# Hosting four input-projection loads instead of two in the first attention of a two-block layer, with the modulation sums read in half-megabyte pieces

## The chip, the cores and the metric

The kernel runs on one core of one Trainium2 chip. The metric is the device time of one execution in microseconds (us), as the median over runs. Three runs of the kernel before gave 2601.82, 2596.1 and 2588.16 us.

## The reference

Two blocks run on 256 tokens of width 2048, in float32. The change lies in the first one:

```python
mod = c_act @ ada_w + ada_b                      # 2048 x 12288: 24 loads of 512 columns
sh1, sc1, g1, sh2, sc2, g2 = split(mod, 6)
u = rms_norm(h, norm_mix_g) * (1.0 + sc1) + sh1
proj = u @ w_in                                  # split into q, k, v, gates of four attentions
o = concat([fox_attention, nsa_attention, dilated_attention, diff_attention])
h = h + g1 * (o @ w_out)
u = rms_norm(h, norm_ffn_g) * (1.0 + sc2) + sh2
h = h + g2 * swiglu(u, ffn_w_gate, ffn_w_up, ffn_w_down)
x = rms_norm(h, final_norm_g)
```

Fox has 7 heads with a cumulated forget gate, the dilated attention (DIL) 9, NSA 8 with three branches (cmp, slc, win) whose results are added under gates, and the differential attention (DIFF) 4 heads of two maps each. A second block (memory attention, chunked attention, an RWKV-like mixer) follows and is not changed.

## The kernel before

**Weights and units.** A weight matrix is cut into loads of 2048 rows by 512 columns (4 MB), a load into four units of 1 MB. SP brings the units in the order of `STREAM` (line 102) into a ring of four; ring slot g is loaded again when unit g is done (line 1760). Every float32 product is made of three: ACT rounds the unit to its high half (`high`, line 1858), DVE subtracts for the low half (`low`, line 2530), and PE takes high x high, high x low and low x high (`unit`, line 2127, with tokens in PSUM rows, 24 products of 512 columns; `unit_features`, line 2143, with features in rows, 48 products of 256 columns). The last third of a unit waits for its low half (line 2136 or 2150).

**Dense stage.** `W_IN_ORDER` (line 98) has the twelve loads of w_in. The first `N_DENSE` = 10 are run one after the other (line 2246). Loads 0 to 7 are feature loads: 0 and 1 fox and dilated queries, 2 NSA queries, 3 DIFF queries, 4 and 5 the keys of 0 and 1, 6 DIFF keys, 7 the NSA keys. Loads 8 to 11 are token loads (gates and values); of load 11 only 288 columns are used (line 95). Beside the units PE makes the compress products of NSA (line 2231).

**ada.** `mod` comes from 24 ada loads: DVE multiplies 16 rows of 128x512 by a scalar of c each and adds them up (`ada_part`, line 2538), and PE sums over partitions with `ada_sum` (line 2183, 8 short instructions). The first `N_FIRST_ADA` = 8 loads come before w_in; POOL fetches them, and the ninth, into two buffers of 4 MB, in halves of 2 MB (line 1783). The loads 8 to 16 use one buffer of 4 MB beside the dense units (line 1803), 4.5 rows in each slot, a slot being the time of one unit from the second load on (lines 227 to 230, 2675). The next three (`N_MID`) come in pieces of two rows (0.5 MB), one buffer, beside the attention: POOL sends a piece when the one before is used (line 1811), `ada_pieces` (line 2563) takes it in the steps of `MID_PIECE` (line 233). The four last run beside the FFN.

**POOL's queue.** In order: the early ada halves, mem to DRAM, cmp_w1 (lines 1797 to 1802, when the 16th transpose round is done), the ada halves of loads 9 to 16, both parts of the mask tables (line 1807), the pieces (line 1809). cmp_w1 is 2 MB, the tables of DIL and cmp 2.1 MB, those of NSA and DIFF 1.6 MB.

**First attention.** `GROUP_SEQ` (line 79) lists seven groups for each of two query tiles: 0 and 1 fox and dilated, 2 slc, 3 win, 4 cmp, 5 and 6 DIFF; 48 units of two heads. In step n (line 2390) PE runs the hosted products of that step, the scores of unit n, the transposes of the probabilities of unit n-2 and the values of unit n-3. DVE (line 2823) adds the mask table and takes the maximum (`score`, L2706, L2710), ACT takes the exponentials; the scores of unit n wait for DVE's L2710 of unit n-1. The planner `plan_hosted` (line 192) spreads the hosted units over the steps by `STEP_MM` (line 189) and with them the halves of their high and low conversions (L2806). Hosted are loads 10 and 11 of w_in and of w_out the half that needs only the fox and dilated heads, which is transposed in steps 20 to 23 (`FD_ROUNDS`). `finish` (line 2729) reads a group's bank four steps after its end. Two rounds of transposes for DIFF run at steps 48 and 49, those for NSA after the loop (line 2432), then the other half of w_out (line 2428 on) and the FFN.

Of the kernel before, what the change touches and what calls it, by code (L numbers as in the profile page):

```python
# [5 lines left out]
P = 128  # L6
SEQ = 256
# [21 lines left out]
N_ADA, N_EARLY, N_FIRST_ADA, N_MID = 24, 17, 8, 3  # L29
# [21 lines left out]
def place(table, *items):  # L51
    at = 0
    for name, n in items:
# [25 lines left out]
GROUP_SEQ = ([(qt, g) for qt in range(TT) for g in (1, 0)] + [(0, g) for g in (2, 3, 4, 5, 6)]  # L79
             + [(1, g) for g in (2, 5, 6, 3, 4)])  # L80
# [17 lines left out]
W_IN_ORDER = (7, 8, 0, 1, 2, 3, 4, 5, 6, 9, 10, 11)  # L98
N_DENSE = 10
# [86 lines left out]
HOSTED_UNITS = [(i, q, 4) for i in range(2) for q in range(4)] + [(2 + nb, q, 2) for nb in range(4) for q in range(2)]  # L186
LAST_HOSTED = HOSTED + len(HOSTED_UNITS)
N_STEPS = N_ATT + 3
STEP_MM = [12] * 8 + [6] * 16 + [7] * 24 + [8] * 3
# [37 lines left out]
ADA_COUNT = [(k + 1) * 9 // 2 - k * 9 // 2 for k in range(32)]  # L227
ADA_END = [next(k for k in range(32) if (k + 1) * 9 // 2 >= 16 * (m + 1)) for m in range(N_EARLY - N_FIRST_ADA)]
ADA_SUM_SLOT = {k + 2: N_FIRST_ADA + m for m, k in enumerate(ADA_END)}
ADA_READ_SLOT = {k + 4: N_FIRST_ADA + m for m, k in enumerate(ADA_END)}  # L230


MID_PIECE = {(2 * i if i < 12 else 26 + (i - 12) * 18 // 11): i for i in range(8 * N_MID)}
MID_SUM = {n + 2: N_EARLY + i // 8 for n, i in MID_PIECE.items() if i % 8 == 7}
FD_ROUNDS, DIFF_ROUNDS = (20, 21, 22, 23), (48, 49)
# [106 lines left out]
def hybrid_blocks(nc, A, out):  # L342

    ctx = ExitStack()
    with ctx:
# [19 lines left out]
        def ada_buf(i):  # L365

            if i % 2 == 0 and i < N_EARLY or N_EARLY <= i < N_EARLY + N_MID:
                return ada_acc
            return ada_tmp[:]

        def ada_bank(i):

            if N_EARLY <= i < N_EARLY + N_MID:
                return TRB
            return OB if i < N_FIRST_ADA or i >= N_EARLY else TRB + 1
# [67 lines left out]
        def ada_piece(i):  # L443

            if i < 12:
                return xn[:, 0, 1024:2048].rearrange("p (k n) -> p k n", n=CH)
            at = xT_flat[:, 3072:4096] if i < 8 * N_MID else xn_flat[:, 2048:3072]
            return at.rearrange("p (k n) -> p k n", n=CH)
# [41 lines left out]
            "tabs_in0", "tabs_in1", "w1_in", "early_in0", "early_in1", "early_in2", "early_in3", "early_used", "mem_saved", "piece_in", "piece_used", "gate_exp", "gate_done", "f_abs", "f_ln", "logf_ready",  # L490
# [16 lines left out]
        def early_of(n):  # L507

            if n >= N_FIRST_ADA:
                return early, 0, N_FIRST_ADA // 2 + n - N_FIRST_ADA  # L510
            return (early2 if n % 2 else early), 2 * (n % 2), n // 2
# [4 lines left out]
        DIFF_AT = [GROUP_END[GROUP_SEQ.index((qt, 6))] + 6 for qt in range(TT)]  # L516
# [94 lines left out]
        def probT(n):  # L611

            at = xn[:, 1, 1024:2048] if n < 36 else xT_flat[:, 2048:3072]
# [1161 lines left out]
        def _(pool):  # L1775

            def early_half(n, half):
                k = slice(half * KT // 2, (half + 1) * KT // 2)
                return pool.dma_start(early[:, k], A["ada_early"][n, half].rearrange("p (k n) -> p k n", n=CH))


            pool.dma_start(mem_x[:, 0], A["mem"][0:P]).then_inc(s_["mem_in"], 16)
            for n in range(N_FIRST_ADA + 1):
                buf, which, _ = early_of(n)
                for half in range(2):
                    if n >= 2:
# [3 lines left out]
                        .then_inc(s_[f"early_in{which + half}"], 16)  # L1790
            def early_loads(first, last):
                with pool.Fori(first, last) as n:
                    for half in range(2):
                        pool.wait_ge(s_["early_used"], n * 2 + (half - 1))
                        early_half(n, half).then_inc(s_[f"early_in{half}"], 16)

# [6 lines left out]
            early_loads(N_FIRST_ADA + 1, N_EARLY)  # L1803

            n_tabs = A["tabs"].shape[1]
# [1241 lines left out]
```

## Time and profile before

| what | value |
|---|---|
| median of three runs | 2596.1 us |
| profiled execution | 2601.68 us |
| its span, first to last instruction | 2599.9 us |
| mean granted clock of TensorE in it | 0.981 |
| instructions | 35147 |
| DMA | 549.44 MB, mean 211 GB/s |

The span is what the rows below are cut from; 1.8 us lie around it. PE is TensorE's matmuls, PEld its weight loads, DVE VectorE, ACT ScalarE, POOL GpSimd, SP SyncE. Granted clock 1.00 is 2.4 GHz, 0.50 is 1.2 GHz; a stretch between the two has parts of both. The reported end of a matmul is modelled and overlaps the next start, so a group's pitch is read from start to start.

### The profile page before, as it was taken

Reading aid. Unit: us, or ns where it says so; the run is one execution under the profiler, and the core shown is the slowest. Engines: PE = TensorE matmul, PEld = TensorE weight load, DVE = VectorE, ACT = ScalarE, POOL = GpSimd, SP = SyncE. Lnnn points to the kernel's source line nnn. Section 1 sums busy time; section 2 is a strip of 40 time slices with the busy share of each in tenths; the row PEclk is TensorE's granted clock in tenths of the full one; section 3 lists DMA queues with packets and bytes.
Section 4 is the critical chain, followed back from the end, with each engine's and each line's share of the span. In section 5 each row is a group of like instructions: output and inputs, shape, how many; then the busy total and the mean of one; then the engine's idle time right before and its main releaser. Section 6 shows DMA issues by size and latency. Waiting matters only on the chain.

```text
span 2599.9 us, 35147 instructions
## 1 busy us (share of the span) xinstructions
PE 2520.6 (97%) x15126; PEld 2030.0 (78%) x15126; DVE 1568.6 (60%) x1843; ACT 1025.7 (39%) x1246; POOL 88.1 (3%) x162
## 2 busy tenths in 40 slices
PE   6999999889899999999999899999999999999999
PEld 3479997767688888888888788887888777777887
DVE  6778884666755555555444665546954454446864
ACT  2033334445443333333333444543654333333332
POOL 0000000000000000000000000001000000000000
PEclk9999999789899999999999999999999999999999
DMA  9988995333366666655555654456655333335654
GB/s 409 427 303 315 349 359 208 123 129 132 135 225 223 229 222 226 226 213 208 179 193 194 251 184 147 177 206 213 226 185 188 125 125 121 127 131 219 253 184 162
DMA packets 77802, 549.44 MB, mean 211 GB/s; under 512 B 8807, under 2 KB 8967, under 8 KB 22737
## 3 DMA queue, kind: packets, MB, share of 16 engines
q1 hardware_dynamic: 56656, 405.36, 43.2%
q0 software_dynamic: 20992, 141.85, 14.4%
q8 instruction: 119, 1.95, 0.3%
q14 instruction: 35, 0.28, 0.0%
HBM read 531.46 MB, written 12.58 MB: 209 GB/s over the span
## 4 chain that ended last, share of the span: by engine, by line
PE 90%; DVE 5%; DMA 3%; ACT 1%; issue 1%; SPq 0%; DVEq 0%; ACTq 0%
PE psum L2138 40%; PE psum L1015 25%; PE psum L2153 7%; PE psum L2211 4%; PE psum L2371 2%; PE psum L2121 2%; DMA weights<-in_loads 1%; DMA xT<-in_loads 1%; PE psum L1143 1%; PE psum L1152 1%; PE psum L1150 1%; PE psum L2193 1%; PE psum L2290 1%; PE psum L2312 1%; DVE arena L2577 1%
## 5 line engine op out<-in xcount | busy, mean ns | idle before, releaser
L1828 ACT ACTIVATE unit_high<-weights 128x1024 fp32r<-128x1024 f32 (+1 forms) x501 | 717.6, 1448 | 1098.7 <-PE psum L2138 612.9
L2533 DVE TENSOR_TENSOR unit_low<-weights,unit_high 128x2048 fp32r<-128x2048 f32 x229 | 524.6, 2291 | 441.3 <-ACT unit_high L1828 440.9
L1388 DVE TENSOR_TENSOR unit_low<-weights,unit_high 128x1024 fp32r<-128x1024 f32 x240 | 289.2, 1221 | 188.8 <-ACT unit_high L1828 188.7
L2138 PE MATMUL psum<-unit_high,z_high 128*128 128x512 f32 x1152 | 290.7, 395 | 1.8 <-DVE arena L2870 1.8
L2138 PE MATMUL psum<-unit_high,z_low 128*128 128x512 f32 x1152 | 284.7, 389 | 0.0
L2138 PE MATMUL psum<-unit_low,z_high 128*128 128x512 f32 x1152 | 284.6, 389 | 0.0
L1015 PE MATMUL psum<-unit_high,z_high 128*128 128x512 f32 x960 | 284.6, 406 | 0.0
L1015 PE MATMUL psum<-unit_high,z_low 128*128 128x512 f32 x960 | 266.9, 394 | 0.0
L1015 PE MATMUL psum<-unit_low,z_high 128*128 128x512 f32 x960 | 263.8, 396 | 1.3 <-DVE unit_low L1388 1.3
L2138 PEld LDWEIGHTS psum<-unit_high,z_high 128*128 128x128 f32 x1152 | 215.8, 190 | 46.4 <-DVE arena L2870 2.2
L2138 PEld LDWEIGHTS psum<-unit_high,z_low 128*128 128x128 f32 x1152 | 216.2, 188 | 45.3
L2138 PEld LDWEIGHTS psum<-unit_low,z_high 128*128 128x128 f32 x1152 | 216.2, 188 | 44.9
L1015 PEld LDWEIGHTS psum<-unit_high,z_low 128*128 128x128 f32 x960 | 179.5, 188 | 40.8 <-issue 1.4
L1015 PEld LDWEIGHTS psum<-unit_low,z_high 128*128 128x128 f32 x960 | 176.3, 188 | 39.6 <-DVE unit_low L1388 2.1
L1015 PEld LDWEIGHTS psum<-unit_high,z_high 128*128 128x128 f32 x960 | 170.9, 188 | 36.0 <-issue 2.0
L1828 ACT ACTIVATE xn<-psum 128x256 f32<-128x256 f32 (+2 forms) x96 | 41.9, 437 | 214.7 <-PE psum L1143 126.5
L2211 PE MATMUL psum<-weights,arena 128*128 128x512 f32 x256 | 115.0, 607 | 6.4 <-DMA weights<-in_loads 5.4
L2555 DVE SCALAR_TENSOR_TENSOR arena<-arena,misc 128x512 f32<-128x512 f32 x135 | 101.4, 751 | 6.4 <-DMA arena<-in_ada_early 1.9
L2211 PEld LDWEIGHTS psum<-weights,arena 128*128 128x128 f32 x256 | 49.0, 194 | 65.4 <-issue 58.7
L1828 ACT ACTIVATE arena<-psum 128x512 f32<-128x512 f32 (+6 forms) x113 | 62.0, 577 | 65.6 <-PE psum L2211 48.9
L2138 PE MATMUL psum<-unit_high,h_high 128*128 128x512 f32 x352 | 87.5, 391 | 0.0
L2138 PE MATMUL psum<-unit_low,h_high 128*128 128x512 f32 x352 | 86.9, 389 | 0.0
(405 smaller groups left out, 2817.0 us busy)
## 6 DMA issues: line engine op xcount, KB each, us to landing
weights<-in_loads SPq DMA_DIRECT2D x380, 1024.0 KB, 4.8
arena<-in_ada_early POOLq DMA_DIRECT2D x26, 2048.0 KB, 11.3
xn<-in_loads POOLq DMA_DIRECT2D x44, 512.0 KB, 5.3
weights<-in_ada_early POOLq DMA_DIRECT2D x8, 2048.0 KB, 21.3
xT<-in_loads POOLq DMA_DIRECT2D x12, 512.0 KB, 3.9
gates_kept<-h POOLq DMA_DIRECT2D x12, 512.0 KB, 3.5
arena<-gates_kept POOLq DMA_DIRECT2D x12, 512.0 KB, 8.5
arena<-in_b_rows POOLq DMA_DIRECT2D x10, 512.0 KB, 6.9
```

What stands on the lines that cost most here:

```text
L1015: ins = mm(psum[:, FILL_BANKS[j % 3]], x[:, 4 * q + k, m * P:(m + 1) * P], w[:, k], start=(q == 0 and i in (0, 12)), stop=(q == 3 and i in ...
L1143: ins = mm(psum[r, 4, u * DH:(u + 1) * DH], Lm[r, u], DD[r, u, 0], start=True, stop=True)
L1150: mm(psum[r, 5, u * C2:u * C2 + DH], DD[r, u, 1], Pm[r, u], start=True, stop=True)
L1388: ins = V.tensor_tensor(ring_lo[:, g % RING, c], ring[:, g % RING, c], unit_hi[:, g % 2, c].bitcast(F32), ALU.subtract)
L1828: return nc.scalar.activation(out_, in_, ACT.Copy, scale=scale)
L2121: ins = nc.tensor.transpose(psum[:, bank, (2 * j + m) * P:(2 * j + m + 1) * P], src[:, m, k * P:(k + 1) * P], ident)
L2138: ins = mm(psum[:, bank + m, 0:width], xk[:, m * P:(m + 1) * P], w[:, k, 0:width], start=(first and i % 8 in (0, 4) and part == 0), stop=( ...
L2153: ins = mm(psum[:, bank + c // 2, (c % 2) * SEQ:(c % 2 + 1) * SEQ], w[:, k, c * P:(c + 1) * P], x[:, k0 + k], start=(first and part == 0 a ...
L2211: ins = mm(psum[:, 2 * (i % 2) + m], memT[:, 4 * q + k, m * P:(m + 1) * P], w[:, k], start=(q == 0 and k == 0), stop=(q == 3 and k == 3), ...
L2371: ins = mm(psum[:, FILL_BANKS[j % 3], 0:width], x[:, 4 * q + k, m * P:(m + 1) * P], w[:, k, 0:width], start=(q == 0 and u in (0, 12)), sto ...
L2533: V.tensor_tensor(ring_lo[:, g % RING], ring[:, g % RING], unit_hi[:, g % 2].bitcast(F32), ALU.subtract)\
L2555: ins = V.scalar_tensor_tensor(acc_, early[:, k], c_act[:, k:k + 1], acc_, ALU.mult, ALU.add)
```

## The change

It hosts four loads of w_in (10, 11, 3, 6) instead of two, and so has eight dense loads; the hosted feature loads are computed with features in rows, two products of 256 columns in place of one of 512. `STEP_MM` becomes twelve products in steps 0 to 31, nine in 32 to 47, eight in 48 to 50 and 24 in a new last step 51. The order of groups is now fox and dilated for both tiles, then (0, cmp), (0, slc), (0, win), (1, slc), (1, win), the four DIFF groups and (1, cmp); `NSA_FIRST` names the branch that writes instead of adding. The transposes for the fox and dilated half of w_out move to steps 28 to 31, those for DIFF to step 50. `N_EARLY` is 8: the ninth early load and the 4 MB buffer are gone, and from the eighth load on all ada rows come as pieces of 0.5 MB: 65 of them (2 or 3 in a slot) beside the dense units, one in each of steps 0 to 14 and 32 to 47, through three buffers. These lie in the first 12 KB per partition of the table area, so POOL loads the tables of DIL and cmp before the pieces and those of NSA and DIFF after piece 79; then the pieces wait for the last hosted unit of w_in and use three other buffers.

```diff
-N_ADA, N_EARLY, N_FIRST_ADA, N_MID = 24, 17, 8, 3
+N_ADA, N_EARLY, N_MID = 24, 8, 12
...
-GROUP_SEQ = ([(qt, g) for qt in range(TT) for g in (1, 0)] + [(0, g) for g in (2, 3, 4, 5, 6)]
-             + [(1, g) for g in (2, 5, 6, 3, 4)])
+GROUP_SEQ = [(0, 1), (0, 0), (1, 1), (1, 0), (0, 4), (0, 2), (0, 3), (1, 2), (1, 3), (0, 5), (0, 6), (1, 5), (1, 6), (1, 4)]
+NSA_FIRST = (4, 2)
...
-W_IN_ORDER = (7, 8, 0, 1, 2, 3, 4, 5, 6, 9, 10, 11)
-N_DENSE = 10
+W_IN_ORDER = (7, 8, 0, 1, 4, 5, 2, 9, 10, 11, 3, 6)
+N_DENSE = 8
...
-N_STEPS = N_ATT + 3
-STEP_MM = [12] * 8 + [6] * 16 + [7] * 24 + [8] * 3
+N_STEPS = N_ATT + 4
+STEP_MM = [12] * 32 + [9] * 16 + [8] * 3 + [24]
...
+SLOT_PIECE = [range(k * 65 // 28, (k + 1) * 65 // 28) for k in range(28)]
+MID_PIECE = {**{n: 65 + n for n in range(15)}, **{32 + k: 80 + k for k in range(16)}}
+ADA_END = [next(k for k in range(28) if 8 * m + 7 in SLOT_PIECE[k]) for m in range(8)]
+ADA_SUM_SLOT = {min(k + 2, 27): N_EARLY + m for m, k in enumerate(ADA_END)}
...
-FD_ROUNDS, DIFF_ROUNDS = (20, 21, 22, 23), (48, 49)
+FD_ROUNDS = (28, 29, 30, 31)
...
-            if i < 12:
-                return xn[:, 0, 1024:2048].rearrange("p (k n) -> p k n", n=CH)
-            at = xT_flat[:, 3072:4096] if i < 8 * N_MID else xn_flat[:, 2048:3072]
+            if i < 80:
+                at = arena[:, 12288 + i % 3 * 1024:12288 + (i % 3 + 1) * 1024]
+            elif i < 8 * N_MID:
+                at = (xT_flat[:, 3072:4096], Wb[:, 1, 3 * UNIT:3 * UNIT + 1024], Wb[:, 1, 3 * UNIT + 1024:4 * UNIT])[i % 3]
+            else:
+                at = xn_flat[:, 2048:3072]
...
             n_tabs = A["tabs"].shape[1]
+            a = N_ALIBI * TAB_W
             pool.wait_ge(s_["early_used"], 2 * N_EARLY)
-            for half, (a, b) in enumerate(((N_ALIBI * TAB_W, n_tabs), (0, N_ALIBI * TAB_W))):
-                nc.gpsimd.dma_start(arena[:, 12288 + a:12288 + b], A["tabs"][:, a:b]).then_inc(s_[f"tabs_in{half}"], 16)
+            nc.gpsimd.dma_start(arena[:, 12288 + a:12288 + n_tabs], A["tabs"][:, a:n_tabs]).then_inc(s_["tabs_in0"], 16)
             for i in range(N_PIECES):
-                if i:
+                if i == 80:
+                    pool.wait_ge(s_["piece_used"], 80)
+                    nc.gpsimd.dma_start(arena[:, 12288:12288 + a], A["tabs"][:, 0:a]).then_inc(s_["tabs_in1"], 16)
+                    pool.wait_ge(s_["unit_done"], HOSTED + 4 * len(HOSTED_LOADS))
+                elif i >= 8 * N_MID:
                     pool.wait_ge(s_["piece_used"], i)
-                else:
-                    pool.wait_ge(s_["cmp_hidden"], 1)
-                if i == 12:
-                    pool.wait_ge(s_["unit_done"], unit_of(PLAN["w_in"][0] + 11, 3) + 1)
+                elif i >= 3:
+                    pool.wait_ge(s_["piece_used"], i - 2)
...
+                if (qt, p) == (0, GROUPS[5][0]):
+                    pe.wait_ge(s_["hosted_free"], 8)
...
+                        if load is not None and load < 8:
+                            for c in range(2):
+                                cs = slice((2 * m + c) * P, (2 * m + c + 1) * P)
+                                ins = mm(bank[:, c * SEQ:(c + 1) * SEQ], w[:, k, cs], x[:, 4 * q + k],
+                                         start=(first and c == 0), stop=last, skip_group_check=True)
...
+                if n == N_ATT + 2:
+                    pe.wait_ge(s_["o_ready"], 2)
+                    pe.wait_ge(s_["pt_ready"], N_ATT)
+                    pe.wait_ge(s_["mod_ready"], N_EARLY + N_MID + 1)
+                    pe.wait_ge(s_["pv_read"], len(GROUP_SEQ) - 1)
+                    transposes(o, KT // 4, 12)
...
-                    if slot < len(ADA_COUNT):
-                        ada_run(ADA_COUNT[slot])
+                    for i in SLOT_PIECE[slot]:
+                        ada_pieces(i)
```

## Rows read from the trace of the kernel before

**Rows 1.** The page: busy time of TensorE, and the chain that ended last, by engine.

```profile
PE 2520.6 (97%) x15126; PEld 2030.0 (78%) x15126; DVE 1568.6 (60%) x1843; ACT 1025.7 (39%) x1246; POOL 88.1 (3%) x162
...
PE 90%; DVE 5%; DMA 3%; ACT 1%; issue 1%; SPq 0%; DVEq 0%; ACTq 0%
```

**Rows 2.** Busy time by stage: us, each engine's busy us, clock, DMA share, GB/s.

```profile
284.00:372.00 88.00, 88.00 (x738) 88.00 (x738) 78.81 (x84) 33.15 (x23) 4.25 (x8) 1.00 0.95 369
372.00:409.00 37.00, 37.00 (x227) 33.28 (x226) 21.48 (x18) 12.41 (x7) 1.57 (x3) 1.00 0.81 313
409.00:452.00 43.00, 41.61 (x216) 31.53 (x214) 22.09 (x64) 20.73 (x53) 2.12 (x4) 0.92 0.49 171
452.00:500.00 48.00, 45.22 (x230) 36.23 (x228) 24.52 (x72) 19.01 (x55) 2.65 (x5) 0.72 0.29 98
500.00:520.00 20.00, 14.80 (x105) 12.54 (x104) 16.17 (x53) 12.35 (x38) 1.59 (x3) 0.91 0.48 166
520.00:560.00 40.00, 35.04 (x170) 25.32 (x172) 23.32 (x72) 16.32 (x53) 2.12 (x4) 0.86 0.34 117
560.00:600.00 40.00, 33.94 (x199) 25.16 (x201) 26.92 (x81) 22.17 (x52) 3.19 (x6) 0.97 0.43 145
600.00:631.00 31.00, 30.45 (x180) 23.85 (x179) 21.72 (x61) 19.82 (x50) 0.53 (x1) 0.95 0.31 103
631.00:700.00 69.00, 56.45 (x237) 44.59 (x237) 49.81 (x55) 30.51 (x40) 0.00 (x0) 0.90 0.39 137
```

**Rows 3.** Waits from 409 to 631 us: who for whom, total us, times, longest.

```profile
DVE arena L2577 <- DMA xT<-in_loads: 15.3, 5, 4.5
...
PE psum L2290 <- DVE misc L2710: 13.8, 9, 3.2
...
DVE arena L2577 <- DMA xn<-in_loads: 2.7, 2, 1.3
```

**Rows 4.** Timeline of TensorE: feature unit, ada sum, token unit, hosted step (start us, us).

```profile
289.96 2.08 PE L2153 MATMUL psum<-z_high,unit_high 128*128 128x256 f32 x16
...
295.71 0.95 PE L2193 MATMUL psum<-cst,ada_tmp 128*128 128x1 f32 x8
...
400.17 1.98 PE L2138 MATMUL psum<-unit_high,z_low 128*128 128x512 f32 x8
401.98 1.98 PE L2138 MATMUL psum<-unit_low,z_high 128*128 128x512 f32 x8
...
412.80 1.19 PE L2371 MATMUL psum<-unit_high,z_high 128*128 128x512 f32 x4
...
416.16 1.19 PE L2371 MATMUL psum<-unit_high,z_high 128*128 128x512 f32 x4
```

**Rows 5.** Timelines at the second load: VectorE's first ada row, TensorE's last third of unit 5.

```profile
181.08 0.48 DVE L2549 TENSOR_SCALAR arena<-arena,misc 128x512 f32<-128x512 f32 x1
...
191.52 1.98 PE L2138 MATMUL psum<-unit_low,z_high 128*128 128x512 f32 x8
```

**Rows 6.** Line views of cmp_w1, the tables, and the piece at 383.8 us: landings.

```profile
L1802 POOL DMA_DIRECT2D xn<-in_cmp_w x2: 522/524/527, 171.4 to 171.9; - x2
...
DMA to landing us min/median/max: 10.9/13.5/16.1
...
DMA to landing us min/median/max: 7.7/11.2/14.6
...
DMA to landing us min/median/max: 17.8/17.8/17.8
```

**Rows 7.** The same view of the 23 pieces sent from 409 to 631 us.

```profile
DMA to landing us min/median/max: 3.7/3.9/7.4
```

**Rows 8.** Timeline of VectorE in a dense slot: low half of a unit, ada rows.

```profile
286.40 2.29 DVE L2533 TENSOR_TENSOR unit_low<-weights,unit_high 128x2048 fp32r<-128x2048 f32 x1 [1.15 <-ACT unit_high L1828]
288.61 3.11 DVE L2555 SCALAR_TENSOR_TENSOR arena<-arena,misc 128x512 f32<-128x512 f32 x4
```

**Rows 9.** Busy time in stretches of 4 us in the attention, columns as in rows 2.

```profile
424.00:428.00 4.00, 3.21 (x16) 2.05 (x14) 2.49 (x8) 1.77 (x5) 0.53 (x1) 1.00 0.88 339
428.00:432.00 4.00, 4.00 (x21) 3.42 (x20) 1.70 (x6) 1.84 (x5) 0.00 (x0) 0.63 0.06 26
432.00:436.00 4.00, 4.00 (x12) 2.68 (x10) 1.53 (x3) 0.26 (x2) 0.53 (x1) 0.52 0.20 37
476.00:480.00 4.00, 4.00 (x12) 2.49 (x8) 0.00 (x0) 0.00 (x0) 0.00 (x0) 0.50 0.00 0
```

More of the change, by code:

```diff
@@ L515, in hybrid_blocks @@
         DIL_AT = [GROUP_END[GROUP_SEQ.index((qt, 0))] for qt in range(TT)]
-        DIFF_AT = [GROUP_END[GROUP_SEQ.index((qt, 6))] + 6 for qt in range(TT)]
+        DIFF_AT = [GROUP_END[GROUP_SEQ.index((qt, 6))] + 5 for qt in range(TT)]
         SB, OBS1 = 2, (5, 7)
@@ L1775, in _ @@
         def _(pool):
-            def early_half(n, half):
-                k = slice(half * KT // 2, (half + 1) * KT // 2)
-                return pool.dma_start(early[:, k], A["ada_early"][n, half].rearrange("p (k n) -> p k n", n=CH))
             pool.dma_start(mem_x[:, 0], A["mem"][0:P]).then_inc(s_["mem_in"], 16)
-            for n in range(N_FIRST_ADA + 1):
+            for n in range(N_EARLY):
                 buf, which, _ = early_of(n)
@@ L1789, in _ @@
                     pool.dma_start(buf[:, k], A["ada_early"][n, half].rearrange("p (k n) -> p k n", n=CH))\
[L1790 to L1795, printed above, removed]
+                        .then_inc(s_[f"ada_in{which + half}"], 16)
             pool.wait_ge(s_["acc_free"], FIRST_ACC["mem"] + 4 + 2)
@@ L2370, in hosted @@
                                 pe.wait_ge(s_["acc_free"], acc + N_DENSE + 1)
-                        ins = mm(psum[:, FILL_BANKS[j % 3], 0:width], x[:, 4 * q + k, m * P:(m + 1) * P], w[:, k, 0:width],
-                                 start=(q == 0 and u in (0, 12)), stop=(q == of - 1 and u in (11, 23)), skip_group_check=True)
+                        bank = psum[:, FILL_BANKS[j % 3]]
+                        first, last = q == 0 and u in (0, 12), q == of - 1 and u in (11, 23)
+                        if load is not None and load < 8:
[3 more added lines that the diff above has]
+                                         start=(first and c == 0), stop=last, skip_group_check=True)
+                        else:
+                            ins = mm(bank[:, 0:width], x[:, 4 * q + k, m * P:(m + 1) * P], w[:, k, 0:width],
+                                     start=first, stop=last, skip_group_check=True)
                         if q == of - 1 and u == 11:
@@ L2602, in _ @@
             scale_tokens(mem_x)
-            for i in range(N_FIRST_ADA):
+            for i in range(N_EARLY):
                 ada_part(0, KT)
```

118 lines of the change are left out of this document (52 added, 66 removed).

## The prediction

> **What bounds the kernel now.** I read the busy times and the chain first, then the table by stage, then the two stages that the change touches instruction by instruction. TensorE is busy for 97% of the span and carries 90% of the chain [rows 1], so only work taken from it, or time in which it is idle or slowly clocked, can move the end. The table by stage [rows 2] shows where such time is. In the dense w_in stage (about 182 to 409 us) it is full and at clock 1.00 from 284 to 409 us, while the DMA engines are 0.95 busy at 369 GB/s and VectorE is busy for 78.8 of 88 us: three resources stand close together. The first attention (409 to 631 us) is the loose part. Over its six rows TensorE is idle for 1.4 + 2.8 + 5.2 + 5.0 + 6.1 + 0.6 = 21 us, and the share of clock not granted, (1 - clock) times the length of each row, adds 3.4 + 13.4 + 1.8 + 5.6 + 1.2 + 1.6 = 27 us. So 48 of 222 us are waste, and 174 us are work at full clock. Part of the idle time starts with the single buffer for pieces of ada: VectorE waits 15.3 + 2.7 us for their landing, and TensorE waits 13.8 us at the scores for VectorE's L2710 [rows 3].
>
> **Part 1: loads 3 and 6 move out of the dense stage.** A unit of a feature load runs from 289.96 to 295.71 us, 5.76 us with its pitch, and a token unit 5.44 us (3 x 1.81 us per 8 products of 512 columns) [rows 4]. Eight feature units leave: -46.1 us. One ada sum, 0.8 us [rows 4], moves from the dense stage to the attention. Dense gross: -46.9 us. The same products and the same sum come back in the attention: +46.9 us. The change pays only by the waste that they fill.
>
> **Part 2: ada in half-megabyte pieces.** The ninth load, in place before the stage, is no longer fetched early, and no buffer of 4 MB is left: three of 0.5 MB take its place.
>
> *Start.* VectorE comes to the first ada product of slot 0 at 181.08 us with its data there; the low half of unit 5 follows in order, and TensorE takes it up at 191.52 us [rows 5]. After the change POOL queues cmp_w1 (2 MB), then the dilated tables (2.1 MB), then pieces 0 to 2 on one queue. cmp_w1 is issued at 171.9 us and lands at 188.0 (16.1 us) [rows 6]. Of the tables the same row group gives 7.7 us for the first transfer, which is this one, and 17.8 us for a piece queued behind 3.7 MB of tables at 383.8 us. So the tables land about 188.0 + 7.6 = 195.6 and piece 0 some 3.7 us later [rows 7], at 199.3 us. Two pieces are 1.2 + 1.5 us with piece 1 landing behind, then 2.2 us for the low half (prices from [rows 8]): 204.6 us. TensorE has waited 204.6 - 191.5 = 13 us, and a half-clock spell after it, 8 us long after a gap of 0.8 us at 426 us [rows 9] but with denser products here, costs some 2 more: +15 us. Ends: +9 (the queue drains at the ceiling because TensorE's stall stops the weights) and +19 (piece 1 contends like the worst row, 7.4 us [rows 7]).
>
> *Rest of the stage.* Per slot VectorE has a low half of 2.2 us and 65/28 = 2.32 pieces of two operations, 3.1 us for four being 1.5 us each: 5.7 us [rows 8], besides blocks and reads. TensorE needs 5.76 us plus 0.8 us for a sum in every third or fourth slot: 6.0. The DMA has to move 1.05 + 2.32 x 0.524 = 2.27 MB, at the 388 GB/s that 369 GB/s at a share of 0.95 give [rows 2]: 5.85 us. Before, it was 2.23 MB with up to 4 MB in flight; now 1.5 MB. Averages still fit, bursts do not. A piece needs 0.3 us to issue after its buffer is freed and lands in 3.7 to 7.4 us [rows 7]: 4.0 to 7.7 us round trip, plus 1.5 us of use, once in three pieces, that is in 1.29 slots. The slot cannot be shorter than (4.0 + 1.5)/1.29 = 4.3 us or (7.7 + 1.5)/1.29 = 7.1 us. In this stage weights are almost always in flight, so I stand near the upper end and take 6.3 us, 0.3 over 6.0, for 24 slots, about +8 us with the catching-up of VectorE after the start. Ends: 0 and 1.1 x 24 = +26 us.
>
> The rows give a median of 3.9 us for a half-megabyte piece, nearly alone on the engines [rows 7]. The Trainium skill, DMA: Bandwidth & Descriptors, section Bandwidth, advises transfers of 1 MiB and more, because a fixed part of about 2 us stands in each; its formula gives 3.2 us here as an estimate, a round trip of 3.5 us and no loss in the later slots, so that the sum would be 8 us lower. The measured 3.9 us is above it, and the measurement decides.
>
> **Part 3: twelve products in each of the first 32 steps.** A step with twelve products of 512 columns and only scores beside them takes 3.4 us now (412.80 to 416.16) [rows 4]. From step 8 to 24 the products double from six, and from 24 to 32 they rise from seven to twelve; then come nine, eight, and a last step of 24 which covers the last eviction. ACT and VectorE get 16 more half-unit conversions (about 1.1 and 1.2 us each, some 36 us in all, covered by TensorE's own longer steps; uncovered they would be the whole 19 us of VectorE). Pieces: 31 in place of 24, 1.5 us each, +10 us on VectorE, which was busy for only 135 of 222 us, the sum of the six rows [rows 2]. With three buffers its 18 us of waiting for pieces [rows 3] have no reason to recur. I leave about 19 of the 48 us of waste: 2 in steps 0 to 7; 6 in steps 8 to 15, where the hosted load has only 288 columns; 3 in 16 to 31; 8 in the last twenty, where a piece in each step, the differential finishes and nine products put VectorE level with TensorE. Gain: -29 us. Ends: -40 (8 us stay) and -8 (40 stay).
>
> **Part 4: small edits.** The new group order, the o transposes at steps 28 to 31 and 50, and cmp as the last group change no instruction's size. One scale factor on an ACT copy is free. Two waits are new. TensorE's scores at step 36 wait for the eighth hosted eviction, made at step 32: free, unless VectorE is behind. POOL holds piece 80 until the 16th hosted unit is done, at the end of step 31, and VectorE wants it in step 32: with 0.5 us to issue and 3.7 to 7.4 us to land [rows 7] against a step of about 4.5 us, up to 3 us of wait with the scores of step 33 behind it; this is in the 8 us of part 3. The other half of the tables (1.6 MB) goes out at step 14 and is wanted at step 20. For the order I take 0; the cover is a 24-product step of 5.4 us, and if it fails, the two transpose rounds cost up to 3 us. The tail (631 to 700 us, [rows 2]) is unchanged, as are the FFN and block 2.
>
> **Sum.** -46.9 + 15 + 8 + 46.9 - 29 = -6 us against the profiled execution's 2601.7 us (span 2599.9 and 1.8 us around it): 2595.7. That execution stands 5.6 us above the median of the three runs, 2596.1, so I predict 2590 us. All good ends: 9 + 0 - 40 = -31; all bad ends: 19 + 26 - 8 = +37.
>
> **Rivals.** *R1, the waste is filled and the pieces keep up.* Start +10, later slots 0 to 4, waste down to 15 us (-33): about -20 us, 2576. For it: with twelve products a step the clock is still 1.00 from 424 to 428 us, five steps into the attention [rows 9], and the averages of part 2 fit. Against it: the start-up order on the queue, which nothing hides.
>
> *R2, the three-piece ring starves VectorE, the slower case.* Place: each slot of the dense stage from piece 3 on. If the round trip is 7.7 us on average, the slot is 7.1 us and the stage loses 26 in place of 8, and the half-clock spells behind such waits take some 4 more: +16 us, 2612. It decides from a round trip of about 6.6 us upwards, where (6.6 + 1.5)/1.29 = 6.3 us. For it: DMA share 0.95 with deep buffers [rows 2]; against it: the stall at the start and the 12 us of the compress products give it time to catch up.
>
> *R3, the clock stays down.* From 476 to 480 us TensorE was busy for 4.00 of 4.00 us with clock 0.50 [rows 9]: in the fox units of the second query tile no gap was needed to hold it low. If the 288-column products beside them do not lift it and more spells follow, 33 of the 48 us stay: +8 us, 2604. By the Trainium skill, TensorE: Matmul & The Clock Gate, section HAM oscillation, it is idle gaps between bursts that drop the clock. As a mechanism here, R4: filled gaps would restore the clock everywhere and leave some 8 us of idle time, -17 us, 2579. The row speaks against the page, since the low clock there outlived a stretch without a gap.
>
> *R5, nothing moves:* gain and loss cancel within 3 us; it lies inside the forecast.
>
> **Chances.** Forecast with R5 (2583 to 2603) 0.40; R1 0.27; R4 0.08; R2 0.15; R3 0.10. Below 0.5% (13 us) a measurement cannot tell this kernel from itself. Faster by over 0.5% (below 2583): R1 and R4, 0.35. Within: the forecast and a part of R3, 0.43. Slower (above 2609): R2 and the rest of R3, 0.22. The range leaves out the far ends: 2562 to 2612; the likeliest case alone is 2583 to 2603.
>
> **What would show it.** The first w_in unit of the next load should show TensorE waiting about 13 us for the low half near 191 us, and VectorE waiting for arena from in_loads there. Pieces should land in 5 to 7 us in the dense stage. Attention should begin near 386 us (before: 409) and last about 240 us, with waste near 19. Attention starting before 375 us would be R1; after 400 us R2. A wait of VectorE for pieces of over 3 us within attention would refute part 3, and a half clock without a gap would confirm R3. If there is no wait at 191 us, the step on the queue order is wrong.

## The result, and the profile after

The changed kernel takes 2616.8 us (median of 8 runs, 2613.9 to 2627.3) against 2595.4 us for the kernel before: a ratio of 1.0086, 95% interval 1.0068 to 1.0104. It is slower by 21 us. The prediction was 2590 us with a range to 2612, so the result fell outside it, on the slow side. Timed once more later, the changed kernel took 2617.1 us, ratio 1.0094 (1.0074 to 1.0115).

The profiled execution took 2623.4 us, with a span of 2621.6 us; before it was 2599.9. The page shows the same work on TensorE and a chain that goes less through it and more through VectorE and the DMA than in [rows 1]:

```profile
PE 2524.9 (96%) x15126; PEld 2036.0 (78%) x15126; DVE 1567.6 (60%) x1851; ACT 1021.1 (39%) x1254; POOL 116.1 (4%) x216
...
PE 85%; DVE 7%; DMA 5%; issue 2%; ACT 1%; POOL 0%; SPq 0%; DVEq 0%; ACTq 0%
```

The table by stage of the changed kernel, with the columns of [rows 2]: us, busy us of TensorE, weight loads, VectorE, ACT and POOL, then clock, DMA share and GB/s. The dense stage ends and attention begins at 395.1 us, which was 409.2.

```profile
182.00:227.00 45.00, 27.45 (x129) 22.91 (x128) 23.83 (x27) 10.72 (x7) 4.76 (x9) 0.83 0.88 322
227.00:284.00 57.00, 57.00 (x601) 56.95 (x601) 41.00 (x51) 19.13 (x17) 8.99 (x17) 0.84 0.76 264
284.00:372.00 88.00, 83.45 (x664) 81.35 (x664) 71.98 (x79) 29.29 (x21) 15.34 (x29) 0.98 0.90 337
372.00:395.00 23.00, 20.26 (x94) 15.81 (x93) 19.17 (x23) 7.50 (x4) 4.75 (x9) 1.00 0.90 341
395.00:409.00 14.00, 14.00 (x62) 10.51 (x62) 10.57 (x24) 5.61 (x16) 1.58 (x3) 0.88 0.80 309
409.00:452.00 43.00, 39.79 (x240) 32.01 (x239) 29.65 (x77) 20.42 (x56) 4.75 (x9) 0.92 0.60 211
452.00:500.00 48.00, 47.43 (x305) 41.89 (x304) 24.63 (x69) 19.57 (x53) 1.06 (x2) 0.86 0.38 139
500.00:520.00 20.00, 20.00 (x160) 17.94 (x160) 11.42 (x37) 9.39 (x29) 0.00 (x0) 1.00 0.39 145
520.00:560.00 40.00, 36.44 (x277) 32.76 (x277) 21.70 (x60) 20.95 (x54) 1.57 (x3) 0.96 0.39 145
560.00:600.00 40.00, 39.76 (x238) 30.55 (x237) 30.30 (x78) 21.50 (x56) 4.23 (x8) 1.00 0.53 185
600.00:650.00 50.00, 43.51 (x215) 33.85 (x214) 37.12 (x94) 24.56 (x56) 2.65 (x5) 0.86 0.39 137
```

Two things are to be seen. From 284 to 372 us TensorE was full before (88.00 of 88); now it is idle for 4.6 us, and for 17.6 us in the row from 182 us on. In the attention, on the other hand, the rows are fuller: TensorE is idle for 14 us (3.2 + 0.6 + 3.6 + 0.2 + 6.5) and loses 20.4 us to the clock (14 x 0.12 + 43 x 0.08 + 48 x 0.14 + 40 x 0.04 + 50 x 0.14), 34.5 us of waste against 48. Attention, from the first hosted product to the first product of the later w_out half, lasts 254.3 us, from 395.1 to 649.4, so its work at full clock is 219.8 us.

The waits say who is late. First the dense stage, 157 to 395 us (who for whom and for what, us in total, times, longest), VectorE and then TensorE:

```profile
DVE arena L2575 <- DMA arena<-in_loads: 18.3, 1, 18.3
DVE ada_tmp L2581 <- DMA arena<-in_loads: 14.4, 9, 3.1
DVE arena L2581 <- DMA arena<-in_loads: 10.9, 7, 3.7
...
PE psum L2131 <- DVE unit_low L2536: 16.4, 3, 14.8
PE psum L2146 <- DVE unit_low L2536: 7.3, 5, 2.8
```

VectorE waits 43.6 us for pieces in these three rows, and behind them in its queue stands the low half of the next unit, for which TensorE then waits 23.7 us. The first of these waits is the one at unit 5, here in the timelines of TensorE and VectorE, and the landings of pieces 0 to 2 in the view of their line:

```profile
205.07 3.52 PE L2131 MATMUL psum<-unit_low,z_high 128*128 128x512 f32 x8 [14.76 <-DVE unit_low L2536]
...
198.13 0.49 DVE L2575 TENSOR_SCALAR arena<-arena,misc 128x512 f32<-128x512 f32 x1 [18.34 <-DMA arena<-in_loads]
...
201.27 1.54 DVE L2581 SCALAR_TENSOR_TENSOR arena<-arena,misc 128x512 f32<-128x512 f32 x2 [1.87 <-DMA arena<-in_loads]
202.73 2.29 DVE L2536 TENSOR_TENSOR unit_low<-weights,unit_high 128x2048 fp32r<-128x2048 f32 x1
```

```profile
DMA to landing us min/median/max: 26.5/29.1/29.9
```

The three pieces are sent by 172.6 us and are there 26.5 to 29.9 us later, because cmp_w1 (2 MB) and the dilated tables (2 MB) stand ahead of them. The third of the unit that waited then runs at half clock: 3.52 us, where the eight products took 1.98 in [rows 5].

In the attention, 395 to 650 us, TensorE's waits are these:

```profile
PE psum L2307 <- DVE misc L2591: 5.6, 2, 3.6
PE psum L2375 <- issue: 3.6, 1, 3.6
PE psum L2186 <- issue: 1.8, 1, 1.8
```

The waits at the scores of [rows 3] (13.8 us) are down to 1.4 us, and VectorE's waits for pieces in the attention (18 us) are gone, as predicted. In their place stand two waits of the transposes (L2307) for the read of an ada sum (L2591), which end at 441 and 605 us, and one before the first w_out product, which ends at 556 us.

### The profile page after: what moved, and what is told of

The parts are those of the page before. It is cut to its first block, busy times and chain, and to the rows that moved or that the text cites. A ratio compares the mean times of both kernels' runs of the same rounds, so it can differ in the third digit from the quotient of the medians.

```text
span 2621.6 us, 35208 instructions
## 1 busy us (share of the span) xinstructions
PE 2524.9 (96%) x15126; PEld 2036.0 (78%) x15126; DVE 1567.6 (60%) x1851; ACT 1021.1 (39%) x1254; POOL 116.1 (4%) x216
## 3 DMA queue, kind: packets, MB, share of 16 engines
q0 software_dynamic: 28768, 141.86, 14.7%
## 4 chain that ended last, share of the span: by engine, by line
PE 85%; DVE 7%; DMA 5%; issue 2%; ACT 1%; POOL 0%; SPq 0%; DVEq 0%; ACTq 0%
PE psum L2131 38%; PE psum L1015 25%; DMA arena<-in_loads 4%; PE psum L2204 4%; PE psum L2375 3%; PE psum L2372 2%; PE psum L2114 2%; PE psum L2146 1%; DVE arena L2581 1%; DMA weights<-in_loads 1%; PE psum L1143 1%; PE psum L2337 1%; PE psum L2285 1%; DVE ada_tmp L2581 1%; PE psum L2307 1%
## 5 line engine op out<-in xcount | busy, mean ns | idle before, releaser
L2536 DVE TENSOR_TENSOR unit_low<-weights,unit_high 128x2048 fp32r<-128x2048 f32 x221 | 506.0, 2290 | 419.7 <-ACT unit_high L1818 419.6
L2114 PE MATMUL psum<-cst,xn 128*128 128x128 f32 x264 | 42.1, 310 | 42.1 <-DVE xn L2497 21.2
```

Of the source, the lines that this page charges most:

```text
L2114: ins = nc.tensor.transpose(psum[:, bank, (2 * j + m) * P:(2 * j + m + 1) * P], src[:, m, k * P:(k + 1) * P], ident)
L2536: V.tensor_tensor(ring_lo[:, g % RING], ring[:, g % RING], unit_hi[:, g % 2].bitcast(F32), ALU.subtract)\
```

## The experiments

A landing is the time from a piece's DMA instruction to its arrival; the round trip of a buffer is the landing and the 0.3 us from the freed buffer to the next instruction. Theory A, formed from the two traces: pieces come late in the dense stage, first because of what stands ahead of them on POOL's queue (theory Q), then because three buffers are too few for the round trip under full DMA (R2 of the prediction); and the attention's gaps are made by the order of VectorE's own queue (theory O). Rivals: DMA volume as such (D), VectorE's volume of work (V), and that the hosting is what costs (H). Each "and" in the table adds to the line above; "after" is the changed kernel.

| run | what differs | us, median | ratio to before | attention begins, ends |
|---|---|---|---|---|
| after again | nothing | 2617.1 | 1.0094 (1.0074 to 1.0115) | 393.6, 640.9 |
| e_tabs_late | after, tables behind piece 64 | 2618.1 | 1.0081 (1.0057 to 1.0105) | 390.0, 644.6 |
| e_tabs_again | the same as e_tabs_late | 2614.8 | 1.0081 (1.0062 to 1.0101) | 388.9, 638.3 |
| e_early | and pieces 0 to 2 first | 2603.7 | 1.0028 (1.0013 to 1.0044) | 376.3, 628.2 |
| e_ring6 | and six buffers | 2592.0 | 0.9985 (0.9971 to 1.0000) | 367.7, 615.8 |
| e_thin | after, a quarter of the bytes of pieces 0 to 64 | 2599.1 | 1.0006 (0.9988 to 1.0023) | 378.3, 626.8 |
| e_ada_alone | after, hosting as before | 2621.7 | 1.0079 (1.0051 to 1.0108) | 424.1, 650.7 |
| e_host2_ring6 | e_ring6, hosting as before | 2606.6 | 1.0032 (1.0012 to 1.0051) | 409.8, 633.5 |
| e_att3 | after, attention's order mended | 2609.1 | 1.0055 (1.0038 to 1.0071) | 395.8, 635.8 |
| e_att | e_ring6, attention's order mended | 2580.7 | 0.9940 (0.9917 to 0.9963) | 372.9, 610.1 |
| e_all | and fewer pieces in the first slots | 2577.2 | 0.9923 (0.9901 to 0.9946) | 365.3, 602.6 |
| e_last | and six buffers to piece 59, one piece in the last slot | 2571.8 | 0.9906 (0.9888 to 0.9924) | 364.4, 601.8 |

**1. The tables.** POOL sends the dilated tables behind piece 64:

```
-            nc.gpsimd.dma_start(arena[:, 12288 + a:12288 + n_tabs], A["tabs"][:, a:n_tabs]).then_inc(s_["tabs_in0"], 16)
             for i in range(N_PIECES):
+                if i == 65:
+                    nc.gpsimd.dma_start(arena[:, 12288 + a:12288 + n_tabs], A["tabs"][:, a:n_tabs]).then_inc(s_["tabs_in0"], 16)
```

> The changed kernel with one difference: the dilated tables go out after piece 64 and no longer ahead of piece 0; the pieces still stand behind cmp_w1. Theory Q (the order on POOL's queue makes the 16.5 us stall of unit 5): piece 0 lands some 7 us earlier, near 191 us in place of 198, the stall of unit 5 falls from 16.5 to about 9 us, attention begins some 8 us earlier (387 in place of 395) and the time is 2609 against 2617 for the changed kernel. Rival D (the weights and the pieces share a DMA that is full, whatever the order): the tables' 2.1 MB only moves to a later place, the stall shrinks but the slots after it lose the same, attention begins at 394 to 396 and the time stays at 2617. Rival V (VectorE's own work is the bound in the dense stage): it catches up with the same backlog, gain under 3 us.

The stall came down from 14.8 to 8.7 us (its row: TensorE's third of unit 5), and attention began 5.1 us earlier, not the 8 us of theory Q: TensorE's other waits in the stage rose from 10.0 to 11.5 us.

```profile
200.49 3.58 PE L2132 MATMUL psum<-unit_low,z_high 128*128 128x512 f32 x8 [8.66 <-DVE unit_low L2537]
```

The median (2618.1) did not move, where theory Q had 2609, so it was timed again beside the changed kernel.

> The kernel of e_tabs_late once more, beside the changed kernel on the same chip: its profile showed attention 5 us earlier, its median (2618) did not. Theory Q: 3 to 7 us under the changed kernel of this call. Rival D: within 2 us of it, the transfer is only moved.

Against the changed kernel timed beside it (2617.1) it was 2.4 us faster, and attention began 4.7 us earlier in its profile (5.1 in the first pair). The stall shrank as theory Q has it; as a time, 2.4 us lies between the two expectations and below what these intervals can tell.

**2. Pieces ahead of cmp_w1**, with the tables behind piece 64 as in e_tabs_late:

```
+            pool.wait_ge(s_["early_used"], 2 * N_EARLY - 1)
+            for i in range(3):
+                piece(i)
             pool.wait_ge(s_["acc_free"], FIRST_ACC["mem"] + 4 + 2)
...
```

> Pieces 0 to 2 are sent as soon as all but the last half of the eighth ada load are used, ahead of the memory's copy and of cmp_w1; the tables go out after piece 64. Theory Q: no stall at unit 5 at all, attention begins 16 to 20 us earlier than in the changed kernel (375 to 379 us), the time is 2597 to 2601. If the slots after it are also late because of the stall (VectorE catching up), another 5 us. Rival D/R2 (a ring of three starves VectorE in every slot): units 6 to 27 still lose some 20 us in all, the start's gain is partly lost: attention at 383 or later, 2606 or more.

The long stall was gone and attention began at 376.3 us, as theory Q expected; the median fell by 13.1 us from the 2616.8 of the changed kernel, to 2603.7, between the two ranges (2597 to 2601, and 2606 or more). TensorE's waits in the dense stage were now many and short, 10.3 us in all:

```profile
PE psum L2166 <- DVE unit_low L2556: 6.2, 6, 1.5
PE psum L2151 <- DVE unit_low L2556: 4.1, 3, 1.9
```

Theory Q holds for the start. What is left is spread over the slots, as R2 says.

**3. Six buffers in place of three** (pieces 0 to 47; the arena has the room until the tables come):

```
+        def piece_slot(i):
+            return i % 6 if i < 48 else i % 3
...
-                at = arena[:, 12288 + i % 3 * 1024:12288 + (i % 3 + 1) * 1024]
+                at = arena[:, 12288 + piece_slot(i) * 1024:12288 + (piece_slot(i) + 1) * 1024]
```

> As the kernel with early pieces, and six buffers in place of three for pieces 0 to 47. Theory R2 (the round trip of a buffer of the ring of three holds the slots of the dense stage): a further 8 to 13 us earlier than with three buffers, attention at 365 to 372, time some 2588 to 2592. Rival D (averages of the DMA bind, not the depth): under 3 us from the three more buffers. Rival V (VectorE's work binds): under 3 us, and its waits for pieces vanish while TensorE still waits for the low half.

Attention began 8.6 us earlier and the median fell by 11.7 us, all within theory R2's ranges; rival D had under 3 us. In the median a piece took longer than with three buffers, and the kernel was faster. The landings of the pieces sent from 215 us to the end of the dense stage (min, median, max), first the changed kernel:

```profile
DMA to landing us min/median/max: 3.6/5.7/8.9
```

with six buffers:

```profile
DMA to landing us min/median/max: 3.8/6.9/11.0
```

and in between, with early pieces and three buffers (e_early), the median was 5.9 us and the longest 13.1.

So it is the depth that counts, not the bytes. By the prediction's formula three buffers cover the median round trip, 6.0 us, since (6.0 + 1.5)/1.29 = 5.8 us is under the slot of 6.0; they don't cover the long ones, up to 9.2 us.

**4. Bytes or VectorE.**

```
-                pool.dma_start(ada_piece(i), src.rearrange("p (k n) -> p k n", n=CH)).then_inc(s_[f"ada_in{i % 3}"], 16)
+                w = CH // 4 if i < 65 else CH
+                pool.dma_start(ada_piece(i)[:, :, 0:w], src.rearrange("p (k n) -> p k n", n=CH)[:, :, 0:w]).then_inc(s_[f"ada_in{i % 3}"], 16)
```

> The changed kernel (three buffers, the old order on the queue), but the DMA of each of the first 65 pieces brings only a quarter of its columns; VectorE works on all of them, on what is there. It leaves out the right values of most ada sums. Theory R2/D (round trip under a full DMA): the loss of the slots after the start falls from 18 us to under 5, landings take 2 to 4 us in place of 5 to 9, attention begins near 378 us (start stall about 13 us because of cmp_w1 and the tables), time 2597 to 2603. Rival V (VectorE's work in the dense stage binds): the landings get shorter, but attention still begins after 388 and TensorE waits for the low half as before; time 2610 or more.

With three buffers, the same VectorE work and a quarter of the bytes, landings took 3.6 us in the median, and after the start TensorE was full where the changed kernel had 83.45 of 88:

```profile
DMA to landing us min/median/max: 2.4/3.6/5.7
```

```profile
284.00:372.00 88.00, 88.00 (x677) 84.61 (x675) 80.19 (x84) 30.91 (x22) 23.39 (x33) 1.00 0.63 224
```

VectorE did 80.2 us of work in those 88 and was not late. That refutes V for the dense stage; the run leaves out the right values of most ada sums, but not the work on them. The stall at the start stayed at 11.3 us, since cmp_w1 and the tables were whole.

**5. Hosting apart from the sums.** The hosting goes back to two loads (ten dense ones), the new way for the ada sums and the new order of groups stay:

```
-N_DENSE = 8
+N_DENSE = 10
...
-STEP_MM = [12] * 32 + [9] * 16 + [8] * 3 + [24]
+STEP_MM = [12] * 8 + [6] * 40 + [8] * 3 + [24]
...
-SLOT_PIECE = [range(k * 65 // 28, (k + 1) * 65 // 28) for k in range(28)]
+SLOT_PIECE = [range(k * 65 // 32, (k + 1) * 65 // 32) for k in range(32)] + [range(0)] * 4
```

> The hosting as in the kernel before (ten dense loads, two hosted, twelve products a step in the first eight steps and then six), with the change's way for the ada sums (eighth load on in half-megabyte pieces over three buffers, 65 pieces in 32 of the 36 slots) and its order of units. Theory A (the ada part costs about 34 us in the dense stage and saves the attention's 18 us of waits for pieces): attention begins near 432 us in place of 409, is 10 us shorter than the 222 us before, and the time is 2605 to 2612; hosting then adds 5 to 12 us more. Rival H (hosting is what costs, since the attention's waste does not fill): this kernel is at 2590 to 2598 and the hosting costs 20 us.

The whole slowdown is there without the extra hosting: 1.0079 against 1.0086. Rival H is refuted, but theory A's sum was off too: the dense stage lost 15 us and not 23 (attention began at 424.1, expected 432), and the attention, which was to shrink by 10 us, grew from 221.6 to 226.5. It was idle for less, 14.7 us against 21, but lost 41.0 us to the clock against 27. Which of the new group order, the new steps and the new pieces raised that loss, no run separates. With late pieces the hosting was worth nothing that can be measured (2621.7 against 2616.8 us). The same question with early pieces and six buffers:

> Early pieces and six buffers as in the run e_ring6 (2592.0), but with ten dense loads and two hosted ones as in the kernel before. Against e_ring6 it prices the hosting alone, where the pieces are not late. Theory F (the hosting fills waste of the attention: without it 41 us of clock are lost there in place of 12): e_ring6 is 15 to 25 us faster, so this kernel takes 2607 to 2617. Rival G (65 pieces in 28 slots in place of 32 and the fuller attention give it back): both within 5 us, 2587 to 2597. Its attention should begin at 392 to 398 us and lose 40 us to the clock, as e_ada_alone did.

Now the hosting was worth 0.9985 against 1.0032, some 12 us; the medians are 14.6 us apart, just under the 15 to 25 of theory F. (The start of attention that was expected, 392 to 398 us, was worked out wrongly: two more loads are 47 us, less what the thinner slots give back; it was 409.8.) The reason is the clock. Over its whole attention the run with two hosted loads lost 37.5 us to half clock, e_ring6 11.9 us, with the same idle time (14.6 and 14.9 us). Nearly all of the difference lies in two parts: the fox units of the second query tile (steps 12 to 15) and the sixteen steps behind them. First the run with two hosted loads:

```profile
462.20:491.20 29.00, 29.00 (x117) 22.95 (x116) 14.58 (x40) 9.34 (x26) 1.06 (x2) 0.61 0.40 147
491.20:552.80 61.60, 59.10 (x305) 46.85 (x304) 29.30 (x112) 30.61 (x95) 1.57 (x3) 0.74 0.26 94
```

then e_ring6 in the same steps, with four:

```profile
426.40:450.90 24.50, 24.50 (x155) 20.58 (x154) 16.52 (x39) 10.39 (x25) 1.06 (x2) 0.93 0.46 155
450.90:528.20 77.30, 73.74 (x578) 66.75 (x577) 39.30 (x121) 38.27 (x105) 1.57 (x3) 0.97 0.39 142
```

That is 11.3 and 16.0 us of lost clock against 1.7 and 2.3. The clock differs between executions (last section), but not by as much: the two profiles with two hosted loads lost 37.5 and 41.0 us in the attention, the seven with four and the old order 8.5 to 20.5. But fewer dense units also mean fewer slots for the same 65 pieces (2.32 in each in place of 2.03), and with three buffers this took back in the dense stage what the attention gained: hosting brought the start of attention forward by 29.0 us with three buffers and by 42.1 us with six, of the 46.9 us that it moves.

**6. The attention's order.** Piece 72 opened its accumulator in step 7 while the sum that frees it stood at the end of TensorE's step 8 (and 88 in step 40 with the sum in 41). VectorE waited there with the next scores, the read of the sum behind. The pieces of a new group now come after the step of the sum, and the four o transposes one step earlier:

```
...
+MID_PIECE = {65 + k: k + 2 * (k > 6) for k in range(15)}
+MID_PIECE.update(zip(range(80, 96), (32, 33, 34, 34, 36, 36, 37, 38, 41, 42, 42, 44, 44, 46, 46, 47)))
...
-FD_ROUNDS = (28, 29, 30, 31)
+FD_ROUNDS = (27, 28, 29, 30)
```

> As e_ring6, with two edits in the attention: no piece stands in the step whose ada sum frees its accumulator (the first piece of the next group comes one step after the sum, so that VectorE does not wait there for TensorE's sum with the next scores behind it), and the four o transposes stand in steps 27 to 30 in place of 28 to 31. Theory O (order within VectorE's queue makes the gaps of 2.0, 3.6 and 3.6 us and the half-clock spells behind them): the three gaps fall under 0.5 us each, the spells at 414, 523 and 575 us (6.8, 6.8 and 3.4 us long) go, the attention is 12 to 17 us shorter than the 248 us of e_ring6, and the time is 2575 to 2580. Rival V (VectorE is simply full in these steps): the gaps move to other steps, gain under 4 us.

The rows of the mechanism in e_ring6: VectorE's first operation of piece 88 waits for the sum (L2206), and TensorE's transposes wait for the read (L2611) behind scores, a low half, a finish and the next piece:

```profile
567.58 0.49 DVE L2595 TENSOR_SCALAR arena<-weights,misc 128x512 f32<-128x512 f32 x1 [1.64 <-PE psum L2206]
...
574.11 0.66 PE L2327 MATMUL psum<-cst,arena 128*128 128x128 f32 x4 [3.61 <-DVE misc L2611]
```

In e_ring6 TensorE waited 5.6 us at the transposes and 3.6 us before the first w_out product, as in the changed kernel. In e_att neither wait is there:

```profile
PE psum L2396 <- DVE unit_low L2823: 3.4, 4, 1.5
PE psum L2207 <- issue: 1.8, 1, 1.8
PE psum L2306 <- DVE misc L2726: 1.2, 2, 0.7
```

The attention shrank from 248.1 to 237.2 us and the median by 11.2 us to 2580.7, just short of the expected 12 to 17 us; the waits for low halves rose from 1.7 to 3.4 us and took some of it. The same edits on the changed kernel with its three buffers:

> The changed kernel with three buffers and its order on the queue as they are, and only the two edits of e_att in the attention. If the order within VectorE's queue made the attention's gaps independently of the dense stage, the gain is what it was with six buffers (11 us): 2604 to 2608, with attention still beginning near 395 us. Rival: with three buffers the two pieces in one step wait for each other's landing, gain under 5 us.

> The changed kernel as it is, as the yardstick of this call: 2612 to 2621 (2616.8 before), attention beginning at 393 to 397 us.

They gained 8.0 us (2617.1 to 2609.1), just short of the expected range, with the dense stage as it was: attention began at 395.8. The gap's cause doesn't depend on the buffers.

**7. The rest of the dense stage.** e_all has fewer pieces in the first slots, `[2, 2, 1, 1, 3, 3, 4]` and then 49 over 21 slots:

> As e_att, with the pieces of the first slots of the dense stage thinned: 2, 2, 1, 1, 3, 3, 4 and then 49 over 21 slots, in place of 65/28 in each. Theory S (what is left of the start loss is 2.45 us of wait at unit 8 and 5 us of half clock behind it, because the queue delivers a piece each 3.8 us there): both go, attention begins 5 to 8 us earlier than the 367.7 us of e_ring6, and the time is 5 to 8 us under that of e_att. Rival: DMA is full over the whole stretch, the same loss turns up at units 10 to 14, gain under 2 us.

Attention began 2.4 us earlier than in e_ring6, where 5 to 8 were expected, and 7.5 us earlier than in e_att, whose dense stage is that of e_ring6: one and the same stage ended 5.1 us apart in two executions. The median fell by 3.5 us, less than expected and inside the intervals of the two. The gap of 2.5 us at unit 8 was gone, but a half-clock spell of 10 us in that stretch stayed. It stands beside the compress products (64 x 15, 0.24 us each) and not behind the gap, for the kernel before has less than full clock there too, in a row without a gap:

```profile
227.00:284.00 57.00, 57.00 (x470) 56.40 (x469) 46.15 (x56) 20.45 (x17) 2.83 (x5) 0.96 0.84 317
```

The last run has six buffers to piece 59 and a single piece in the last slot:

> As e_all, with six buffers for pieces 0 to 59 (not 47) and only one piece in the last slot of the dense stage, so that the last ada sum of the stage (slot 27) finds its accumulator made. Theory O: the wait of 2.9 us at that sum goes, and with it the 6.8 us half-clock spell behind it (3.4 us lost): 4 to 6 us under e_all, 2571 to 2574. Rival D (full DMA at the end of the stage, 0.93 of the time): the pieces themselves come late there, the wait moves to another slot, gain under 1.5 us.

2571.8 us, 5.4 us under e_all (the two intervals overlap), and no wait of TensorE for VectorE is left from 157 to 364 us. This version is faster than the kernel before by 0.94% (interval 0.76 to 1.12%). Its rows beside those of [rows 2] and of the changed kernel above:

```profile
182.00:227.00 45.00, 45.00 (x443) 41.08 (x443) 38.76 (x42) 16.77 (x11) 7.92 (x15) 0.95 1.01 384
227.00:284.00 57.00, 57.00 (x486) 56.40 (x484) 48.32 (x62) 20.45 (x17) 10.57 (x20) 0.95 0.89 329
284.00:364.00 80.00, 80.00 (x587) 76.23 (x585) 73.29 (x78) 28.57 (x21) 14.78 (x28) 1.00 0.97 372
```

## Why the prediction was wrong

The prediction had -6 us for the span and the profiled execution has +21.7: a miss of 28 us, in an execution that stands 6.6 us above its median. By stages, attention misses by 15 us, the dense stage with what stands ahead of it by 10, the tail and the rest by 3. Two steps failed, and both left out waits that stand in single slots or steps: the +8 us for the later dense slots, and in the attention the order of the pieces, which part 4 priced at 0.

**The dense gross (-46.9) held.** 409.2 less 46.9 is 362.3 us for the start of attention; e_last, whose dense stage has no gap, has it at 364.4. So the changed kernel loses 395.1 - 364.4 = 30.7 us there, where the prediction had 15 + 8 = 23 over 362.3.

**The start (+15) was right in place and size.** 14.8 us of wait and 1.5 us of half clock behind it, 16.3 us; the low half was taken up at 205.1 us, predicted 204.6 (the prediction's own terms add up to 204.2). The step on the queue order was confirmed by e_early. The Trainium skill, DMA: Bandwidth & Descriptors, section Two DMAs through the same engine are not ordered, says that within one queue of a DMA engine descriptors start in order; the landings of 26.5 to 29.9 us agree.

**The rest of the stage (+8) was too small: this is the first step that failed.** It measured 30.7 - 16.3 = 14 us. The round trip was estimated well (3.9 to 9.2 us, median 6.0; the prediction took 4.0 to 7.7 us). Two things were missed. The prediction took an average of the slot times, but the waits fall in single slots: 8.9 us of TensorE's 23.7 us of waiting are outside the long one. And this term gave the clock nothing: from 227 to 284 us TensorE is busy for 57.00 of 57.00 us at clock 0.84, where e_last has 0.95, which is 57 x 0.11 = 6 us. R2 had the right mechanism, too few buffers, but not its condition, a mean round trip of 6.6 us or more; its price of 26 us was 12 too high. The size of a piece was not what cost here: with six buffers of the same half megabyte most of the loss went, while the median landing grew. The Trainium skill, DMA: Bandwidth & Descriptors, section Bandwidth, advises transfers of 1 MiB and more; no run here tried them.

**The attention was the second failure.** Its work at full clock came out at 219.8 us, close to the 174 + 46.9 of the sum. The waste was to fall from 48 to 19 us and fell to 34.5 us in the profiled execution and, by the same sum over the other profile of the same kernel, to 25.4 us (16.9 idle, 8.5 clock). Cut at the scores of steps 8, 16 and 32, the waste was 2.2, 13.4, 5.3 and 13.5 us in the first and 2.1, 6.1, 6.4 and 10.8 in the second, where part 3 left 2, 6, 3 and 8. Part 3 was right that the waits for pieces would go and those for the scores shrink (to 1.4 us). What it left out is in part 4, where the new order was priced at 0: a group's first piece stands a step ahead of the sum that frees its accumulator (gaps of 2.0 and 3.6 us), and the first w_out product waits 3.6 us for the o transposes, whose low half stands behind a finish on VectorE. The prediction asked only about the waits that the change names, and not about an accumulator used by two groups in turn. Mended, this gave 8 to 11 us, and the attention of e_att3 lasts 239.9 us with 18.4 us of waste, the "about 240" and the 19 of the prediction. It had looked for the trouble at piece 80, where no wait appeared.

**The tail** (631 to 700 us before), left at 0, took some 2 us more, and 1 us came after it. With -1.4 us ahead of the dense stage, -12.7 us in it, +32.8 us in the attention, +2.1 and +1.0, the sum is +21.8 us; the two spans differ by 21.7 (2621.6 - 2599.9).

**The range** was cut on one side only. It was said to leave out the far ends, but its low end, 2562, lies below the sum with all good ends (2596.1 - 31 = 2565), while its high end, 2612, left out all that the bad ends give, +37 or 2633. The measured 2617 lies there.

**The rivals.** R1 was wrong in this kernel. Its 2576 us came out in e_all and e_last (2577.2 and 2571.8), where both its conditions hold: the pieces come in time, and the attention's waste is 15.4 us in e_last; it takes the other order on the queue, six buffers and the mended order of the attention. R3's mechanism is real: in the fox units of the second query tile TensorE had no gap (0.0 us idle) and yet lost 9.2 us to the clock in the kernel before and 6.8 us in the changed one, whose row is

```profile
472.00:476.00 4.00, 4.00 (x19) 4.00 (x19) 3.49 (x8) 2.82 (x7) 0.01 (x1) 0.50 0.00 0
```

It was smaller in other executions with four hosted loads (1.7 us in the second of the changed kernel, 3.4 in e_last). R4, filled gaps restore the clock everywhere, is refuted by the rows of e_last above: from 182 to 284 us it is busy for 45.00 of 45.00 and 57.00 of 57.00 us, with no wait since 157 us, and the clock is 0.95 in both. The Trainium skill, TensorE: Matmul & The Clock Gate, section HAM oscillation, puts a fallen clock down to idle gaps between bursts of work; these rows show that such gaps are not the only cause. In sixteen steps of twelve products full work did go with full clock; a stretch of them in e_last:

```profile
452.00:500.00 48.00, 48.00 (x392) 44.10 (x392) 25.65 (x84) 23.81 (x68) 0.00 (x0) 1.00 0.41 151
```

## What to carry to other kernels

Buffers for a stream are counted from the landing time under the load of that very stage, plus use, and from the long landings rather than the median. A queue is read from its head: what is ahead of the first piece is paid by the engine that waits in order. Before a schedule is called free, follow each accumulator and bank from its last reader to its next writer, on both engines' orders. And a move of work into idle time is worth only what it does not take from the stage it leaves: here fewer dense slots had to carry the same pieces, and the gain of some 12 us appeared only when that stream was deep enough.

## What the runs showed of the hardware

The same kernel lost different time to the clock in two executions whose three largest waits of TensorE in the attention were the same: 20.5 us in the attention of the first profile, 8.5 us in that of the second, whose row for the stretch of the lowest clock is

```profile
452.00:500.00 48.00, 47.63 (x346) 42.28 (x345) 26.78 (x75) 20.91 (x57) 1.06 (x2) 0.96 0.37 136
```

against 0.86 above. What decides between them stays open. So a single profile can't price a part of the attention to better than about 10 us here; the medians of the two timings, 2616.8 and 2617.1 us, agree far better.

Half clock came without a gap ahead of it. In e_last TensorE had no idle time at all from 157 to 364 us; the clock fell beside the 64 x 15 compress products:

```profile
222.00:232.00 10.00, 10.00 (x147) 9.96 (x144) 7.13 (x10) 0.00 (x0) 2.11 (x4) 0.50 0.98 388
```

And doubling the pieces in flight raised their median landing from 5.7 to 6.9 us, at DMA shares of 0.90 and 0.93 from 284 us on, while the stage got shorter.
